# Transposing raw activations amid the projections, and taking the down products of two experts behind the next two's up products, in a two-layer RWKV, attention and MoE trunk on one Trainium2 core

## The reference, cut to what matters

```python
def _rms_norm(x, g):
    y = xf * lax.rsqrt(jnp.mean(xf * xf, axis=-1, keepdims=True) + NORM_EPS)
    return (y * g.astype(jnp.float32)).astype(x.dtype)
...
for i in range(DEPTH):                       # DEPTH 2, h is (512, 1024)
    hn = _rms_norm(h, norm_mix[i])
    h = h + (_rwkv7_time_mix if i % 2 == 0 else _stick_breaking_attention)(hn, ...)
    h = h + _memory_cross_attention(_rms_norm(h, norm_cross[i]), mem_k, mem_v, ...)
    h = h + _hierarchical_moe(_rms_norm(h, norm_ffn[i]), ...)
return _rms_norm(h, norm_final)
...
def _hierarchical_moe(h, wg, bg, we, be, w1, w3, w2):   # 4 groups of 8 experts, 2 chosen
    g_logits = (t @ wg).astype(f32) + bg
    e_logits = ((t @ we).astype(f32) + be).reshape(-1, G, E)
    ...
    hid = silu(t @ w1[gi]) * (t @ w3[gi])    # 1024 -> 256, one product for each expert
    y = y + (hid * gate) @ w2[gi]            # 256 -> 1024
```

## Time and profile before

| | |
|---|---|
| runs | median 1984.23 us (1982.92 to 1988.35, three runs) |
| profiled execution | 1989.41 us, its span on the core 1987.6 us |
| PE, PEld, DVE, ACT, POOL busy | 1640.4, 857.0, 630.9, 402.6, 232.6 us |
| granted TensorE clock, mean | 0.933 |
| 559.0 to 647.0: memory products and `rwo` | in the 87.0 us from 560 PE is busy 86.2 |
| 647.0 to 659.0: cross0 norm | PE 8.5 of 12.0, clock 0.72 |
| 805.0 to 848.0: ffn0 norm and routing | PE 18.5 of 43.0, DVE 27.2, clock 0.64 |
| 864.0 to 1098.0: experts of layer 0 | PE 197.3 of 234.0, DMA engines busy 0.95, 391 GB/s |
| 1299.0 to 1440.0: stick-breaking loop | PE 94.0, DVE 111.8, ACT 62.5, POOL 65.0 of 141.0 |
| 1655.0 to 1698.0: ffn1 norm and routing | PE 18.6 of 43.0, DVE 27.2, clock 0.64 |

### The profile page before, as it was taken

How to read it: one execution, slowest core, us unless ns; L and a number is a source line. 1 busy time by engine, 2 the same in 40 slices (tenths; PEclk the granted TensorE clock), 3 DMA queues, 4 the chain that set the end, 5 groups by cost and what they waited for, 6 DMA issues and landing times.

```text
span 1987.6 us, 30436 instructions
## 1 busy us (share of the span) xinstructions
PE 1640.4 (83%) x12857; PEld 857.0 (43%) x12857; DVE 630.9 (32%) x1096; ACT 402.6 (20%) x753; POOL 232.6 (12%) x322
## 2 busy tenths in 40 slices
PE   5999978887899999589787499967698995787781
PEld 2444477776554454234333244433344543333330
DVE  6111855553550131522111300068701214321113
ACT  2003244543300120110000200044301202010001
POOL 2000132320000000011110100044400000111101
PEclk8999999999899999789899699998899997799996
DMA  6136000000541500669998612210015006599994
GB/s 213 43 127 206 1 4 5 4 4 4 201 159 43 211 1 0 257 262 407 420 421 344 216 52 75 85 43 0 0 43 194 18 0 249 211 405 421 420 399 149
DMA packets 82068, 313.85 MB, mean 158 GB/s; under 512 B 18089, under 2 KB 19169, under 8 KB 57185
## 3 DMA queue, kind: packets, MB, share of 16 engines
q1 hardware_dynamic: 70432, 286.95, 36.9%
q0 software_dynamic: 11520, 25.19, 3.5%
HBM read 305.81 MB, written 35.39 MB: 172 GB/s over the span
## 4 chain that ended last, share of the span: by engine, by line
PE 59%; DMA 10%; DVE 10%; issue 6%; ACT 2%; POOL 1%; SPq 1%; DVEq 0%; POOLq 0%; ACTq 0%; PEldq 0%
PE PS L479 15%; PE PS L465 13%; PE PS L1883 10%; PE PS L919 8%; DMA arena<-in_moe_w 4%; DMA ring<-in_moe_w 4%; PE PS L1908 3%; DVE arena L1409 2%; PE PS L421 2%; PE PS L1231 1%; PE PS L1205 1%; PE PS L1454 1%; DVE arena L407 1%; DVE arena L1420 1%; PE PS L1038 1%
## 5 line engine op out<-in xcount | busy, mean ns | idle before, releaser
L465 PE MATMUL PS<-arena,ring 128*128 128x512 f32 (+1 forms) x1024 | 414.5, 567 | 0.0
L479 PE MATMUL PS<-ring,arena 128*128 128x512 f32 x704 | 305.2, 595 | 0.7 <-ACT arena L1372 0.7
L465 PEld LDWEIGHTS PS<-arena,ring 128*128 128x128 f32 x1024 | 195.2, 191 | 216.4 <-issue 211.9
L479 PEld LDWEIGHTS PS<-ring,arena 128*128 128x128 f32 x704 | 134.5, 191 | 169.7 <-issue 168.6
L1883 PE MATMUL PS<-ring,arena 128*64 128x512 f32 x512 | 123.7, 638 | 22.9 <-DMA ring<-in_moe_w 18.9
L1883 PE MATMUL PS<-arena 128*64 128x512 f32 x512 | 125.0, 644 | 21.3 <-DMA arena<-in_moe_w 14.0
L919 PE MATMUL PS<-ring 64*64 64x64 f32 (+1 forms) x3072 | 97.9, 236 | 19.1 <-issue 14.9
L421 PE MATMUL PS<-ident,arena 128*128 128x128 f32 x208 | 52.1, 405 | 71.8 <-DVE arena L407 66.4
L485 ACT ACTIVATE arena<-PS 128x512 f32<-128x512 f32 (+1 forms) x64 | 36.5, 570 | 366.5 <-PE PS L465 366.5
L1891 DVE TENSOR_TENSOR arena<-PS,arena 128x256 f32<-128x256 f32 x32 | 13.6, 424 | 279.9 <-ACT arena L1888 279.9
L919 PEld LDWEIGHTS PS<-ring 64*64 64x64 f32 x3072 | 84.0, 135 | 25.0 <-issue 20.4
(11 more groups left out here) (261 smaller groups left out, 1980.4 us busy)
## 6 DMA issues: line engine op xcount, KB each, us to landing
arena<-in_moe_w SPq DMA_DIRECT2D x96, 1024.0 KB, 15.1
ring<-in_moe_w SPq DMA_DIRECT2D x96, 1024.0 KB, 18.2
ring<-in_sb_wqkv SPq DMA_DIRECT2D x6, 2048.0 KB, 8.9
ring<-in_xa_wkv SPq DMA_DIRECT2D x4, 2048.0 KB, 15.7
ring<-in_xa_wq SPq DMA_DIRECT2D x4, 2048.0 KB, 8.5
ring<-in_xa_wo SPq DMA_DIRECT2D x4, 2048.0 KB, 13.7
h<-in_x SPq DMA_DIRECT2D x8, 512.0 KB, 5.3
ring<-in_rw_wr SPq DMA_DIRECT2D x2, 2048.0 KB, 13.7
```

The costliest lines, as they stand in the source:

```text
L465: ins = pe.matmul(PS[:, g % NBANK, 0:n], ring[:, u % RING, k, P * (j % 4):P * (j % 4) + P], xt[:, k, 0:n], start=(k == 0), stop=(k == KC - 1))
L479: ins = pe.matmul(PS[:, g % NBANK, :], xt[:, k, P * t:P * t + P], ring[:, (u0 + half) % RING, k, :], start=(k == 0), stop=(k == KC - 1))
```

## The change

1. **Late scaling.** The norms cross0, ffn0, mix1, cross1, ffn1 turn raw `h` (`late_turn`) in blocks of one 128x128 transpose each, over four PSUM banks (three for ffn), and ACT and DVE write each one out times the gain (`late_evac`). For cross and ffn this stands in the second half of the output projection before it: tile t-1 is turned in the middle of the group of tile t, after its fourth matmul of eight, and the last tile behind the projection. For mix1 it follows the MoE of layer 0. The row scale is applied to results: in the scale of the softmax's Exp (an operand that is a tile, where a constant stood), in the two Sigmoids of the stick-breaking loop (the same), in `sv`'s copy, and in `sk`'s copy, which goes from ACT to DVE and multiplies by a row that four small products spread over the partitions.
2. **Logits** are made in token rows, eight matmuls for each tile behind the group, in the projection `xo` (`route_logits`). DVE scales them and adds the bias, a chain of 67 steps. The normed rows for memory are made by ACT after all squares.
3. **Table loads.** Small operations on the tile `warm` bring ACT's tables in earlier (Sqrt at the start, ahead of the squares of each late norm and of the final one; Exp behind the late norm).
4. **Experts.** The order on PE is `up(n)`, turn hidden n-1, turn rows n+1, `down(n-1)`, all pairs written out, with waits on ACT and DVE to match. SP's order from pair 2 on is up 4, up 3, down 2, down 3, up 5, down 4, up 6, down 5, ..., up 15, down 14, down 15.

```diff
+        def late_turn(pe, name, t, ready):
+            ready(pe, t)
+            for k in range(KC):
+                n = LATE0[name] + KC * t + k
+                depth = 3 if name[:3] == "ffn" else 4
+                if KC * t + k >= depth:
+                    late_out(pe, n - depth)
+                pe.transpose(PS[:, late_bank(name, n), 0:P], h[:, t, k::KC], ident[:, :]).then_inc(S("late_turned"), 1)
+
+        def late_evac(eng, name, t, dst, which):
+            for k in range(which, KC, 2):
+                n = LATE0[name] + KC * t + k
+                eng.wait_ge(S("late_turned"), n + 1)
+                g = gainT[:, GAIN[name], k:k + 1]
+                d, v = dst[:, k, P * t:P * t + P], PS[:, late_bank(name, n), 0:P]
+                if which == 0:
+                    eng.activation(d, v, ACT.Copy, scale=g).then_inc(S("late_act"), 1)
+                else:
+                    eng.tensor_scalar(d, v, g, None, ALU.mult).then_inc(S("late_vec"), 1)
+
+        def late_act(act, name, tn, dst, tile_ready):
+            act.activation(warm[:, :], gn_eps[:, :], ACT.Sqrt).then_inc(S("table_warm"), 1)
+            for t in range(NT):
+                tile_ready(act, t)
+                if t < NT - 1:
+                    square(act, name, h, tn, t)
+                late_evac(act, name, t, dst, 0)
+            square(act, name, h, tn, NT - 1)
+            root(act, name)
...
@@ project_tok @@
+                        if within and half == 1 and t and k == KC // 2 - 1:
+                            within(t - 1)
                     ins.then_inc(S("proj_filled"), 1)
+                    if after and half == 1 and t:
+                        after(t - 1)
...
@@ cross_pe @@
-            project_tok(pe, FIRST[xo], UNITS.index(xo), oT, lambda e, k: group_evacuated(e, FIRST[xv] + k))
+            project_tok(pe, FIRST[xo], UNITS.index(xo), oT, lambda e, k: group_evacuated(e, FIRST[xv] + k),
+                        within=lambda t: late_turn(pe, ffn, t, h_tile_ready(xo)),
+                        after=lambda t: route_logits(pe, l, t))
@@ cross_act @@
-                                   bias=xmax[:, x % 2, t:t + 1], scale=XSCALE,
+                                   bias=xmax[:, x % 2, t:t + 1], scale=tscale[:, 0, t:t + 1],
@@ sb_act @@
-                    act.activation(fail[n % NBUF][:, T - nn:T], PS[:, n % NT, 0:nn], ACT.Sigmoid, scale=-HD ** -0.5)\
+                    act.activation(fail[n % NBUF][:, T - nn:T], PS[:, n % NT, 0:nn], ACT.Sigmoid,
+                                   scale=tscale[:, 0, n % NT:n % NT + 1])\
...
@@ moe_route_act @@
-            norm_act(act, f"ffn{l}", h, tnE, h_tile_ready(f"xo{l}"))
-            xT_evac(act, f"ffn{l}", xTE, 0)
...
+            late_act(act, f"ffn{l}", tnE, xTE, h_tile_ready(f"xo{l}"))
+            act.activation(warm[:, :], gn_eps[:, :], ACT.Exp).then_inc(S("table_warm"), 1)
+            act.wait_ge(S("norm_recip"), NIDX[f"ffn{l}"] + 1)
+            for t in range(NT):
+                act.activation(tnE[:, t, :], h[:, t, :], ACT.Copy, scale=rstd[:, t:t + 1]).then_inc(S("norm_rows"), 1)
             act.wait_ge(S("route_a"), 2 * l + 1)
             act.activation(sc[:, :, 0:G], mel2[:, :, 0:G], ACT.Exp).then_inc(S("route_exp"), 1)
...
@@ moe_pe @@
+            for n in range(NPE):
+                up_pair(n)
+                if n:
+                    turn_hid_of(n - 1)
+                if n + 1 < NPE:
+                    turn(n + 1)
+                if n:
+                    down_pair(n - 1)
+            turn_hid_of(NPE - 1)
+            down_pair(NPE - 1)
```

More of the change, by code:

```diff
@@ L383, in trunk @@
         TILE0 = {n: sum(c for _, c in NORMS[:j]) for j, (n, _) in enumerate(NORMS)}
-        TPOSE0 = {n: KC * j for j, (n, _) in enumerate(NORMS)}
+        TPOSE0 = {"mix0": 0, "mem": KC}
+        LATE = ["cross0", "ffn0", "mix1", "cross1", "ffn1"]
+        LATE0 = {n: NT * KC * j for j, n in enumerate(LATE)}
+        ROWS0, _rows = {}, 0
+        for _name, _tiles in NORMS:
+            if _name not in LATE or _name[:3] == "ffn":
+                ROWS0[_name] = _rows
+                _rows += _tiles
         GAIN = {"mix0": 0, "cross0": 1, "ffn0": 2, "mix1": 3, "cross1": 4, "ffn1": 5, "mem": 6}
@@ L391, in norm_act, with square, root @@
                 tile_ready(act, t)
-                act.activation(tn[:, t, :], src[:, t, :], ACT.Square, accum_out=sumsq[:, t:t + 1])\
-                    .then_inc(S("norm_squares"), 1)
+                square(act, name, src, tn, t)
+            root(act, name)
+        def square(act, name, src, tn, t):
+            act.activation(tn[:, t, :], src[:, t, :], ACT.Square, accum_out=sumsq[:, t:t + 1])\
+                .then_inc(S("norm_squares"), 1)
+        def root(act, name):
+            nt = dict(NORMS)[name]
             act.wait_ge(S("norm_mean"), NIDX[name] + 1)
@@ L398, in norm_vec, with row_scales @@
         def norm_vec(vec, name, src, tn):
+            row_scales(vec, name)
+            for t in range(dict(NORMS)[name]):
+                vec.tensor_scalar(tn[:, t, :], src[:, t, :], rstd[:, t:t + 1], None, ALU.mult)\
+                    .then_inc(S("norm_rows"), 1)
+        def row_scales(vec, name):
             nt = dict(NORMS)[name]
@@ L405, in norm_vec @@
             vec.wait_ge(S("norm_recip"), NIDX[name] + 1)
-            for t in range(nt):
-                vec.tensor_scalar(tn[:, t, :], src[:, t, :], rstd[:, t:t + 1], None, ALU.mult)\
-                    .then_inc(S("norm_rows"), 1)
         def norm_pe(pe, name, tn):
@@ L467, in project_T, with project_tok @@
                 ins.then_inc(S("proj_filled"), 1)
-        def project_tok(pe, g0, u0, xt, ready, tiles=NT):
+        def project_tok(pe, g0, u0, xt, ready, tiles=NT, within=None, after=None):
             for half in range(2):
@@ L491, in evac_tok, with add_to_h @@
                                    ACT.Copy).then_inc(S("proj_out_A"), 1)
-        def add_to_h(vec, g0, ready=None):
+        def add_to_h(vec, g0, ready=None, between=None):
             for half in range(2):
@@ L497, in add_to_h @@
                         ready(vec, t)
+                    if between and half == 1 and t:
+                        between(t - 1)
                     v = h[:, t, 512 * half:512 * half + 512]
@@ L1293, in cross_vec @@
                     vec.tensor_copy(probT[x % 2][:, m, :], PS[:, 6 + m, :]).then_inc(S("x_probT"), 1)
-            add_to_h(vec, FIRST[f"xo{l}"])
+            add_to_h(vec, FIRST[f"xo{l}"], between=lambda t: late_evac(vec, f"ffn{l}", t, xTE, 1))
         tnS = at(0, [NT, C])
@@ L1311, in trunk @@
         vs = at(33, [NT, P])
+        mix1_row = at(32, [T])
+        mix1_diag = at(32.5, [NT, P])
         NU = 2 * NT
         def sb_proj_pe(pe):
-            norm_pe(pe, "mix1", tnS)
-            project_T(pe, FIRST["sq"], UNITS.index("sqkv"), xTS, T, lambda e, k: xT_there(e, "mix1", k))
+            for t in range(NT):
+                late_turn(pe, "mix1", t, lambda e, t: e.wait_ge(S("h_moe0"), t + 1))
+            project_T(pe, FIRST["sq"], UNITS.index("sqkv"), xTS, T, lambda e, k: late_there(e, "mix1", k))
+            pe.wait_ge(S("mix1_diag"), NT)
+            for t in range(NT):
+                ins = pe.matmul(PS[:, 4, P * t:P * t + P], ones[:, :], mix1_diag[:, t, :], start=True, stop=True)
+            ins.then_inc(S("mix1_spread"), 1)
             project_T(pe, FIRST["sk"], UNITS.index("sqkv") + 2, xTS, T, lambda e, k: None)
@@ L2008, in moe_vec @@
             vec.nop().then_inc(S("ye_v"), 1)
-            turned(0, 0)
-            last_peeled(vec, body)
+            turned(0)
+            for n in range(NPE):
+                vec.wait_ge(S("sig_ready"), NPE * l + n + 1)
+                if n:
+                    vec.wait_ge(S("hid_turned"), NPE * l + n)
+                silu_half(vec, P).then_inc(S("silu_ready"), 1)
+                vec.wait_ge(S("silu_ready"), NPE * l + n + 1)
+                hid_out(vec, P).then_inc(S("hid_ready"), 1)
+                if n + 1 < NPE:
+                    turned(n + 1)
+                if n:
+                    rows(n - 1)
+            rows(NPE - 1)
         def further(eng, l, body):
@@ L2220, in _ @@
             post_vec(vec)
-            add_to_h(vec, FIRST["rwo"], x_back)
+            add_to_h(vec, FIRST["rwo"], x_back, lambda t: late_evac(vec, "cross0", t, xTX, 1))
             for l in range(2):
                 if l == 1:
-                    norm_vec(vec, "mix1", h, tnS)
-                    xT_evac(vec, "mix1", xTS, 1)
+                    sb_proj_vec(vec)
                     sb_vec(vec)
-                    add_to_h(vec, FIRST["so"])
+                    add_to_h(vec, FIRST["so"], between=lambda t: late_evac(vec, "cross1", t, xTX, 1))
                 cross_vec(vec, l)
```

264 lines of the change are left out of this document (133 added, 131 removed), and 2 rows, old and new, of the table PLAN.

## The result

The changed kernel took 2023.53 us (median of four runs, 2016.38 to 2032.88) against 1984.32 (four runs, 1982.92 to 1988.35). The ratio is 1.0197, 95% interval 1.015 to 1.0244: **some 2% slower**, outside the range that the prediction gave. One run of the kernel before in the second group of experiments, of 4686 us, was slow and is left out.

What follows compares the result with a forecast made beforehand. No engine bounds the whole, each stage has its own limit, and weights bound the experts' stage. The terms -4.6 - 5.8 - 2.9 + 9.4 - 1.1 = -5.0, from 1984.2, give 1979 us, range 1962 to 1992.

Steps and rivals of the forecast that it cites:

- Experts, for each layer: Experts' stage: bound by weights from the first up products on; last up weights 5.0 us earlier, stage -1.9 a layer.
- the Sigmoids: Stick-breaking loop: scale from a tile, 0 in the main sum; as a rival, chance 0.12, +11.5 us, 1990.
- the breaks at double cost: Rival, chance 0.13: a bank's round amid projection matmuls takes 1.3 us, not 0.81; +14, 1993.
- That the down products go behind the next up products buys little: Experts' stage: waits filled were under a wait for weights; if PE bound it, 0.8 for each of 16 pairs, -13.
- cross0 and cross1: Norms ahead of cross-attention: -4.6 and -5.8 us, with 2.4 left behind the projection and three tiles of 1.65 inside.
- Softmax: Cross-attention: table load saved, 0.6 each time, against Exp scales from a tile, at most 1.4 for both layers; together 0.
- Transposes and logits inside `xo`: Output projection before routing: three tiles of transposes, 6.3 us, and three of logits, 6.3; +12.6 a layer.
- Routing: Table 31.6 us after the start of xo's last addition (E), against 42.1: -10.5 a layer; rows before Exp cost 3.7.
- The first gather: Behind the routing table: the gather meets weights in the queues; +4.5 us a layer, between 0 and 6.5.
- mix1: Norm behind layer 0's experts: -4.0 us to the projection, +1.1 for spreading products; -2.9 in all.
- Final norm: Last norm: loses its table load of 1.28 us on the path, less a hop; -1.1.
- cheap breaks: Rival, chance 0.22: transposes and logits hide among projection matmuls, gather shares DMA engines; 1955 to 1965, say 1962.

Runs made afterwards that it cites:

- fetch_ahead: The changed kernel with GpSimd issuing the gather of pair n+3 ahead of the scatter of pair n; 1964.88 us, ratio 0.9906, and again 1963.91 us, 0.9875.
- Exp first: fetch_ahead with the Exp of the group logits ahead of the four normed rows on ACT; 1956.84 us, ratio 0.9853.
- all three edits: fetch_ahead with the Exp ahead of the rows, w13x held until the first gather landed, and all logits behind the projection; 1964.38 us, ratio 0.9885.

## Why the prediction was wrong

It said 1979, in a range of 1962 to 1992, with the experts at -1.9 a layer; 2023.5 came, with the experts at +31.9 and +31.4.

**The step that failed** is in "Experts, for each layer": "the stage is bound by weights from the first `up` on, and the loads that wait for it keep their places behind it". That was asked of SP's queue alone. POOL's queue, with its gathers and scatters, was never followed, although gave the time of a gather as 10.0 in the median: between `down(n)` and the turn of n+3 stand 0.70 (copy), 0.93 (hops), 1.01 (scatter), 0.31 and then the gather, 13 us in all with one of 10.0, against the 7.0 of one `up` in the new order. In the trace of before the first part of it stood already (`down(0)` ended at 869.73, the gather behind its scatter was issued at 872.71, 3.0 later). 3.0 and 10.0 less 7.0 is a wait of 6 in each of 13 pairs, 78 us a layer; measured were 59.6, as five of the 13 waits were of 2.0 to 2.5 and the others of 4.4 to 6.6, for which the traces give no reason. None of the rivals had this wait; the two that ended slower, the Sigmoids and the breaks at double cost, did not come.

**"That the down products go behind the next up products buys little"** was right in size for the order itself, once its wait is gone: 0.9906 against 0.9914 without it.

Of the other steps, measured in the changed kernel:

- *cross0 and cross1*, -4.6 and -5.8: from the first product of `rwo` and of `so` to the first product of cross-attention, -5.8 and -8.9 (67.1 to 61.3, 70.3 to 61.4). The other 1.7 of the -7.5 in the table arose ahead of `rwo`, where fetch_ahead, with the same code, has none of it: luck of the execution. Behind the projection 2.2 us are left (648.53 to 650.75), 2.4 was forecast. The transposes inside were cheaper than 1.65: the timeline has them without any wait for a bank,

```profile
627.22 1.47 PE L474 MATMUL PS<-ident,h 128*128 128x128 f32 x8
628.53 7.03 PE L549 MATMUL PS<-ring,arena 128*128 128x512 f32 x16
```

  so 1.31 a tile to the next product. The three tiles are thus 1.0 cheaper, which accounts for cross0. In cross1 another 1.9 are luck: `so` of the kernel before began at a granted clock of 0.79 (1437.72 to 1447) and took 57.2 us to E where `rwo` took 55.1; after, it began at 1.00.
- *Softmax*, 0: cross-attention 0 gained another 1.0 (749.86 to 741.38, less the 7.5).
- *Transposes and logits inside `xo`*, +12.6: +9.2 (`xo` from the last product of cross-attention to E: 55.0 before, 64.2 after). Three tiles of logits were counted there, and only two stand ahead of E: the third follows the last group. Each took 1.87 and 1.70 to the next product, forecast 2.1. The transposes, 1.9, forecast 2.1, did wait for their three banks as the prediction had it:

```profile
800.80 0.64 PE L474 MATMUL PS<-ident,h 128*128 128x128 f32 x3 [0.24 <-ACT arena L484]
801.62 0.50 PE L474 MATMUL PS<-ident,h 128*128 128x128 f32 x2 [0.18 <-DVE arena L486]
```

- *Routing*, table done at E + 31.6: E + 32.0. The wait of DVE for the Exp behind the four rows on ACT is there, shorter than the forecast 3.7. The logits were ready at E + 7.0 and not at E + 5.1, since the third tile's stand ahead of them and the last tile's took 3.47:

```profile
812.47 4.25 ACT L1708 ACTIVATE arena<-h,rstd 128x1024 f32<-128x1024 f32 x4
816.63 0.20 ACT L1710 ACTIVATE arena<-arena 128x16 f32<-128x16 f32 x1
```

```profile
816.93 0.17 DVE L1743 TENSOR_REDUCE masks<-arena 128x4 f32<-128x16 f32 x1 [2.38 <-ACT arena L1710]
```

  In layer 1 the wait was 3.12. Exp first brought the table 3.8 and 3.2 forward, and 2.2 and 2.9 with w13x held back as well, so the forecast 3.7 is of the right size.
- *The first gather*, +4.5: from its issue to the turn 7.8 us against 3.6, +4.2, in layer 1 8.0 against 4.2, +3.8, and 3.6 again in layer 0 with w13x held back. The Trainium skill, "DMA: Bandwidth & Descriptors", Queues, rings and completion order, describes the engines as going round their queues packet by packet. By that the prediction had +2 to +3.5 as its estimate; both layers are above it, the second by little, so the backlog ahead of the gather seems to count here.
- *mix1*, -2.9: -3.8 to the first product, and +1.1 in the projections with the spreading products (169.75 to 170.85), forecast -4.0 and +1.1. *Final norm*, -1.1: -2.0. *Sigmoids*, 0: the loop took 133.9 before and 131.0 after, and 131.3 and 133.4 in two other traces of the same code, so a cost of their scale from a tile does not show.

With the gather repaired the profiled execution took 1965.3, against 1989.4 before: 24.1 less where the sum has 5.0 (by the ratios of the medians, 19 and 25). By the places in its trace, some 9 of the 19 between are in cross-attention and `xo` of the two layers (fewer logits ahead of E, at a lower price, and 1.0 a layer in the softmax), 4 in the cross norms (1.9 of it the slow start of `so` before), 2.6 in the stages of experts, 2.6 in the stick-breaking loop, which other traces of the code do not bear out, 1.4 in the final norm; the rest cancels.

So the number of the "cheap breaks" rival (1962; its terms add up to 1955 to 1962, not to 1965) fits the repaired kernel, and the range would have held it, but its terms do not: a tile took 1.31 and 1.9 and not 1.16, a tile of logits 1.70 and not half of 2.1, and the first gather cost +4.2 and +3.8 and not 2 to 9 less in sum. Part of that fit is luck.

## What to carry to other kernels

When a product is moved in one engine's order, list every in-order queue that holds a wait on it, the scatters and gathers of GpSimd as much as the loads of SP, and ask what stands behind that wait and how much work is left between its release and its next use. If that is less than the steps up to the transfer and the transfer's own time (7 us of `up` against 3 and a gather of 7 to 11 here), the queue must be moved along with the product: here two numbers made a 2% loss into a gain of 1%. And bring a chain's small step (an Exp of 0.2) ahead of bulk work on its engine, and keep prefetch of what is not yet needed (w13x) from standing ahead of the transfer that everything waits for: together about another 1%.

## What was not expected of the hardware

- A gather of 128 rows was there 3.6 us after its issue with w13x held back, 7.8 with w13x in SP's queue, and landed in 9.85 in the middle of the stage.
- The same logits record of 36 columns took 0.117 us amid large products, at a granted clock of 1.00 (805.40 to 807.10), and 0.206 in one piece behind the projection, at 0.52 (809.91 to 823.10); the same piece took 0.173 a record at 0.63 with all three edits. The lower clock is thus most of the difference. PE's stage of routing in the changed kernel, 805 to 850, ran at 0.54:

```profile
805.00:850.00 45.00, 14.99 (x72) 12.89 (x72) 25.05 (x102) 9.84 (x16) 2.88 (x3) 0.54 0.72 291
```

  Small products were cheapest here where PE was busy anyway.
- A wait costs more than itself. After a wait of 5.58 us for a gather the eight transposes took 1.97 and not 1.04, and the down product 5.06 and not 3.65: 2.3 us more on top of the wait, 0.4 of it, in such a pair. The granted clock was 0.65 from 886.15 to 892.95, behind the wait, and 1.00 from 868.63 to 873.10, where there was none.
- ACT's table load took 1.28 us and the next function began at once (811.07, then 812.36). The Trainium skill, "ScalarE: Activation LUTs", What ACT_TABLE_LOAD costs, adds a drain of 1.38 to a switch of tables; no row here shows one, behind the load or ahead of it (the operation before ended at 811.04).
